# Value products of attention in two 64-query halves with the 64 columns of the own head, and input panels up to 512 columns wide

## What is computed

```python
# mixers of the first block (shortened)
p = rms_norm(x, mix_norm) @ w_in            # 512 x 2208
na:   softmax over a neighbourhood (mask and bias), q and k normed per head
mla:  latents -> w_uq, w_ukv -> heads of 96, rope on 32 of them
diff: w = softmax(q1 k1 + bias) - lam * softmax(q2 k2 + bias), per head
gqa:  4 query heads, 2 key/value heads, axial rope
out = einsum('bhqk,bkhd->bqhd', p, v)       # the value product of each head
```

## Time and profile before

| | |
|---|---|
| median of three runs | 2552.68 us (2552.34 to 2555.12) |
| profiled execution | 2552.25 us, its span 2550.5 us |
| PE, PEld, DVE, ACT busy | 97%, 80%, 51%, 36% of the span |
| projection, layers 0 and 1 | 376.03 to 503.53, 1449.67 to 1576.28 |
| attention, layers 0 and 1 | 503.53 to 672.97, 1576.28 to 1745.15 |

### The profile page before, as it was taken

How to read it: one execution, slowest core, us unless ns; L and a number is a source line. 1 busy time by engine, 2 the same in 40 slices (tenths; PEclk the granted TensorE clock), 3 DMA queues, 4 the chain that set the end, 5 groups by cost and what they waited for, 6 DMA issues and landing times.

```text
span 2550.5 us, 35687 instructions
## 1 busy us (share of the span) xinstructions
PE 2467.1 (97%) x14276; PEld 2041.9 (80%) x14276; DVE 1301.8 (51%) x2078; ACT 920.7 (36%) x1399; POOL 20.5 (1%) x14
## 2 busy tenths in 40 slices
PE   8999999999999999999999999999999999999898
PEld 7888889866778888888888898667788888778686
DVE  5434453468654344564344453785543446573464
ACT  4222233466432222332222335664321224343522
POOL 1000000000000000010000000000000000000000
PEclk9999999999999999999999999999999999999989
DMA  7333233100133333342332321002333324221001
GB/s 218 89 101 99 83 106 94 44 8 10 50 83 94 96 100 88 101 132 84 106 99 81 109 77 44 18 1 66 83 88 102 102 82 135 81 85 50 1 8 62
DMA packets 330945, 201.42 MB, mean 79 GB/s; under 512 B 9872, under 2 KB 328304, under 8 KB 330448
## 3 DMA queue, kind: packets, MB, share of 16 engines
q1 hardware_dynamic: 330288, 195.68, 26.6%
q0 software_dynamic: 544, 4.18, 0.5%
HBM read 197.74 MB, written 2.10 MB: 78 GB/s over the span
## 4 chain that ended last, share of the span: by engine, by line
PE 88%; DVE 5%; ACT 3%; DVEq 2%; issue 1%; DMA 0%; ACTq 0%; SPq 0%
PE bank L863 71%; PE bank L1056 3%; PE bank L1089 3%; PE bank L1029 2%; PE bank L1042 2%; PE bank L1337 1%; PE bank L980 1%; DVE w_lo L1995 1%; ACT w_hi L1486 0%; PE bank L992 0%; DVE top L2367 0%; DMA raw<-in_ffn_w_gate 0%; PE bank L1404 0%; DVEq L2389 0%; DVE bank L2373 0%
## 5 line engine op out<-in xcount | busy, mean ns | idle before, releaser
L863 PE MATMUL bank<-h_hi,w_hi 128*128 128x512 f32 x1640 | 642.9, 392 | 9.6 <-DVE h_lo L2006 5.9
L863 PE MATMUL bank<-h_hi,w_lo 128*128 128x512 f32 x1640 | 639.8, 390 | 0.0
L863 PE MATMUL bank<-h_lo,w_hi 128*128 128x512 f32 x1640 | 639.7, 390 | 0.0
L1995 DVE TENSOR_TENSOR w_lo<-raw,w_hi 128x2048 fp32r<-128x2048 f32 (+2 forms) x198 | 408.3, 2062 | 206.2 <-ACT w_hi L1486 204.1
L1486 ACT CAST w_hi<-raw 128x2048 fp32r<-128x2048 f32 (+2 forms) x198 | 340.2, 1718 | 383.4 <-PE bank L863 347.9
L863 PEld LDWEIGHTS bank<-h_hi,w_hi 128*128 128x128 f32 x1640 | 308.9, 188 | 82.6 <-issue 12.1
L863 PEld LDWEIGHTS bank<-h_hi,w_lo 128*128 128x128 f32 x1640 | 308.7, 188 | 64.7
L863 PEld LDWEIGHTS bank<-h_lo,w_hi 128*128 128x128 f32 x1640 | 308.9, 188 | 63.6 <-issue 0.2
L1527 ACT ACTIVATE probs<-probs 128x512 f32<-128x512 f32 x88 | 55.6, 632 | 680.7 <-DVE probs L2088 680.7
L863 PE MATMUL bank<-hid_hi,w_hi 128*128 128x512 f32 x704 | 273.9, 389 | 0.0
L863 PE MATMUL bank<-hid_lo,w_hi 128*128 128x512 f32 x704 | 273.9, 389 | 0.0
(11 more groups left out here) (413 smaller groups left out, 2701.4 us busy)
## 6 DMA issues: line engine op xcount, KB each, us to landing
raw<-in_ffn_w_gate SPq DMA_DIRECT2D x88, 512.0 KB, 4.0
raw<-in_ffn_w_up SPq DMA_DIRECT2D x88, 512.0 KB, 5.2
raw<-in_w_in SPq DMA_DIRECT2D x64, 512.0 KB, 4.6
raw<-in_ffn_w_down SPq DMA_DIRECT2D x64, 384.0 KB, 3.9
raw<-in_ffn_w_down SPq DMA_DIRECT2D x64, 320.0 KB, 3.3
raw<-in_w_out SPq DMA_DIRECT2D x24, 512.0 KB, 4.5
na_bias<-in_na_rel POOLq DMA_DIRECT2D x2, 1792.0 KB, 9.9
wide<-in_x SPq DMA_DIRECT2D x2, 1024.0 KB, 6.2
```

The source lines that it names most:

```text
L863: last = pe.matmul(to, left[a](k), right[b](k), start=(k == 0 and a + b == 0), stop=(k == n - 1 and a == 1))
L1995: dve.tensor_tensor(w_lo[:, at, 0:n], raw[:, at, 0:n], w_hi[:, at, 0:n].bitcast(F32), ALU.subtract)\
```

## The change

*Panels.* `IN_BLOCKS` has five blocks of up to 512 columns (four of 512, one of 416; the last joins `NA_V` and `DF_V`). Each is loaded and used as two panels of 4 row tiles (`KB`), still ten panels in all. PE adds both panels of a block in bank t, so that bank t is held over two panels, and ACT copies 512 (416) columns once per block. In ACT's order the copies of turns and the roots now stand ahead of the copies of the panel, and the split of panel n + 2 waits by itself until PE has done panel n. In DVE's order `seg_scale` stands ahead of the split. The products of the first panel need row tiles 0 to 3 alone.

*Value products.* `weigh` makes each product as two, with 64 queries stationary each, written to partitions 0 to 63 and 64 to 127 of the bank; only the 64 columns of the own head move. Results lie where they lay.

```diff
-IN_CHUNKS = [(NA_QK, PW), (NA_QK + PW, PW), (GQ_QK, PW), (GQ_QK + PW, PW), (C_Q, PW), (C_Q + PW, B_IN - PW),
-             (DF_QK, PW), (DF_QK + PW, PW), (NA_V, PW), (DF_V, PW)]
+IN_BLOCKS = [[(NA_QK, 2 * PW)], [(GQ_QK, 2 * PW)], [(C_Q, B_IN)], [(DF_QK, 2 * PW)], [(NA_V, PW), (DF_V, PW)]]
+N_IN = 2 * len(IN_BLOCKS)
+N_COPY = len(IN_BLOCKS) * T
+KB = KD // 2
...
@@ pe, project
+                        if part == 0 and block:
+                            pe.wait_ge(proj_copied, at_layer(l, N_COPY, (block - 1) * T + t + 1))
+                        product(bank[t][:, 0:w], h_parts(slice(t * P, (t + 1) * P), part * KB),
+                                w_parts(slot(l, i), KB, w, slice(None)), KB,
+                                operand(l, 1) + part * KB if block == 0 and t == 0 else None,
+                                begin=(part == 0), end=(part == 1)).then_inc(proj_done, 1)
-                        if m == 1:
+                        if m == 2:
                             sums_of_squares(norm_at(l, MIX_NORM))
...
+            def weigh(to, share, value, begin, end):
+
+                for half in range(2):
+                    last = pe.matmul(to[half * HD:(half + 1) * HD], share[:, half * HD:(half + 1) * HD], value, start=begin, stop=end)
+                return last
...
@@ pe, attention
-                                last = pe.matmul(bank[PAIR_MIXED][:, j * P:(j + 1) * P],
-                                                 pair_probsT(p)[:, j, t * P:(t + 1) * P],
-                                                 values(mixer, heads[j], t), start=(t == 0), stop=(t == T - 1))
+                                o = j * P + value_half(mixer, heads[j])
+                                last = weigh(bank[PAIR_MIXED][:, o:o + HD], pair_probsT(p)[:, j, t * P:(t + 1) * P],
+                                             values(mixer, heads[j], t), t == 0, t == T - 1)
...
@@ act, project: behind the turn copies and the roots
+                    for t in range(T) if part else ():
+                        act.wait_ge(proj_done, at_layer(l, N_PROJ, n * T + t + 1))
+                        o = 0
+                        for a, w in IN_BLOCKS[block]:
+                            last = act.activation(proj[:, t, a:a + w], bank[t][:, o:o + w], ACT.Copy, scale=rstd_tok[:, t:t + 1])
+                            o += w
+                        last.then_inc(proj_copied, 1)
+                    if n + 2 < N_IN:
+                        act.wait_ge(proj_done, at_layer(l, N_PROJ, (n + 1) * T))
+                        split(l, PAN_IN + n + 2, KB * IN_WIDTH[(n + 2) // 2])
...
```

More of the change, by code:

```diff
@@ L767, in _ @@
                 load_ffn(l, 1)
-                for n, piece in enumerate(IN_CHUNKS):
-                    load_columns(l, PAN_IN + n, A["w_in"], [piece])
+                for n in range(N_IN):
+                    load_columns(l, PAN_IN + n, A["w_in"], IN_BLOCKS[n // 2], n % 2 * KB, KB)
                 take(l, PAN_LAT)
@@ L852, in spread_roots, with product @@
                 last.then_inc(spread_done, 1)
-            def product(to, left, right, n, ready=None, hid=None):
+            def product(to, left, right, n, ready=None, hid=None, begin=True, end=True):
                 for k in range(n):
@@ L862, in product, with h_parts @@
                     for a, b in ((0, 0), (0, 1), (1, 0)):
-                        last = pe.matmul(to, left[a](k), right[b](k), start=(k == 0 and a + b == 0),
-                                         stop=(k == n - 1 and a == 1))
-                return last
-            def h_parts(cut=slice(None)):
-                return [lambda k, x=x: x[:, k, cut] for x in (h_hi, h_lo)]
+                        last = pe.matmul(to, left[a](k), right[b](k), start=(begin and k == 0 and a + b == 0),
+                                         stop=(end and k == n - 1 and a == 1))
+                return last
+            def h_parts(cut=slice(None), k0=0):
+                return [lambda k, x=x: x[:, k0 + k, cut] for x in (h_hi, h_lo)]
             def w_parts(at, k, n, cut, a=0):
@@ L932, in project @@
             def project(l):
-                for n, (a, w) in enumerate(IN_CHUNKS):
-                    i = PAN_IN + n
+                for n in range(N_IN):
+                    i, w, (block, part) = PAN_IN + n, IN_WIDTH[n // 2], divmod(n, 2)
                     for t in range(T):
@@ L1592, in project @@
                 act.drain()
[L1593 to L1600 removed]
+                for n in range(N_IN):
+                    block, part = divmod(n, 2)
                     for t in range(T):
@@ L2257, in project @@
             def project(l):
-                for n in range(len(IN_CHUNKS)):
-                    if n + 2 < len(IN_CHUNKS):
-                        split(l, PAN_IN + n + 2, KD * IN_CHUNKS[n + 2][1])
+                for n in range(N_IN):
                     for g in GROUPS:
```

42 lines of the change are left out of this document (16 added, 26 removed).

## The result

| | before | after |
|---|---|---|
| median of 4 runs, us | 2553.80 | 2508.95 |
| lowest to highest, us | 2552.34 to 2555.12 | 2506.54 to 2510.63 |
| profiled execution (span), us | 2552.25 (2550.5) | 2510.63 (2508.8) |
| projection, layer 0 / 1, us | 127.50 / 126.61 | 116.31 / 115.10 |
| attention, layer 0 / 1, us | 169.48 / 168.89 | 159.86 / 159.51 |

The ratio is 0.9824, with a 95% interval from 0.9807 to 0.9841: 1.8% faster, where 1.8% was forecast (2507). The kernel before has one more execution here (2554.91) than stood ahead of the prediction. Stage lengths are distances between first matmuls of stages. The stages in the table give back 43.4 us of the span; 2.2 us of that are lost in the first feed-forward, where this execution had 3.4 us of half clock from 28.4, ahead of all that the change touches.

What follows compares the result with a forecast made beforehand. TensorE (PE) was taken as the bound, with a matmul in flight for 97% of the span. Projection 22.7, attention 21.2 and L1244 1.5 sum to 45.4 us; 2552.25 less that gives 2506.9, forecast 2507, range 2498 to 2517 (0.60).

Steps and rivals of the forecast that it cites:

- Prices: Projection matmuls, start to start: 0.2266 us for 512 columns, 0.1866 for 416; wider panels save 9.5 us per layer.
- Projection, 11.4 and 11.3 us less: Input projection of layers 0 and 1: cheaper matmuls and fewer waits save 22.7 us together, bounds 18 to 28.7.
- The stall: Projection, ahead of panel 6: PE idles about 3.3 us until DVE's subtraction, which stands behind the gqa scaling.
- Pairs: Attention value products: a two-head pair saves 0.55 or 0.70 us, a `diff` pair 0.28 or 0.13, after drains.
- Attention, 10.6 us less: Attention, per layer: 12.6 us of halves' gain comes through, less two more clock falls of 1.0 each; 21.2 over both.
- Steps 17 to 25: Attention from 572 to 613, PE and DVE each waiting for the other: 1.2 of 3.6 us comes through.
- steps 26 to 38: Attention from 613 to 657, PE busy 43.8 of 44 us, DVE 33.9: 3.8 of 5.0 us comes through.
- L1244: Value products of one attention of the second block: 1.5 us saved, bounds -1 and 2.
- Swallowed: Rival, attention: DVE swallows PE's gain, leaving 22.7 and at most 8 us; 2522 to 2530 us, chance 0.17.
- All of it: Rival, whole change: no projection stall or fall (28.7), PE's full 35.8 in attention, 2.0 more; 2486 us, chance 0.11.
- Halves in turn: Rival, value products: halves follow one another, 0.43 us per product instead of 0.2233; 2642 us, chance 0.05.
- The clock: Rival, attention: clock stays at half rate, some 80 us a layer for half of attention; 2590 us, chance 0.03.

Runs made afterwards that it cites:

- e6: Changed kernel with each 512 (416) column projection product issued as two matmuls of 256 and 256 (256 and 160) columns: 2515.87 us, ratio 0.9856.
- e3: Changed kernel with DVE's subtraction for panel 6 made after the first of four gqa token tiles instead of after all four: 2499.34 us, ratio 0.9789.
- e11: Changed kernel with both edits, each wide product as two matmuls and panel 6's subtraction after the first gqa token tile: 2515.39 us, ratio 0.9848.
- e5: Changed kernel, but attention issues all key tiles of the first 64 queries, then all of the other 64: 2524.13 us, ratio 0.9884.
- e1: Changed kernel with value products of full width as before; panels and new ACT and DVE orders stay: 2529.52 us, ratio 0.9905.
- e2: Kernel before with value products in halves alone, panels untouched: 2531.08 us, ratio 0.9916.
- e8: Changed kernel, value products in halves, with the gain product and rotation of mla's q and k left out on DVE: 2486.09 us, ratio 0.9742.
- e7: Changed kernel with full-width value products as in e1 and the gain product and rotation of mla's q and k left out: 2514.14 us, ratio 0.9845.
- e4: Changed kernel, each value product as one with 128 queries stationary and only the own head's 64 columns moving: 2537.74 us, ratio 0.9929.

## Why the prediction was right, point by point

- **Prices.** 512 columns 0.2267 (0.2266 said), 416 columns 0.1889 (0.1866 said, on a straight line between rows). Right, and e6 shows that the price is a matter of matmuls' number: two for one costs 114.3 - 105.2 = 9.1 us a layer by these steps, 8.8 us as measured.
- **Projection, 11.4 and 11.3 us less.** 11.2 and 11.5. The stall was 3.3 by hand and 2.87 idle in the trace, with the releaser that was named; the half clock was 444.8 to 451.6, as long as before. Layer 1 had half of it, 3.4 us at 1499.5, as it had before. That the clock fell at all, and for as long, was the dearest case in layer 0: behind the same stall it cost nothing, 1.5 or 2.8 us in other traces (see the order on DVE), so hitting 116.3 there is in part luck. e3 took both away and left 5.1 us beside the matmuls' 105.2; the working had 11.2 - 3.3 - 3.0 = 4.9. So the terms are shown, not only the total. What the working did not say is that the stall hangs on the width: without the width there is no stall either (e6, e11), so of the 9.5 us of cheaper matmuls the changed kernel keeps 2.9 and 4.1.
- **Pairs.** 1.15 for 32 matmuls was said and found; a two-head step is 0.56 shorter, 0.55 was said, and the 0.25 allowed for two drains is borne out twice, by 4.20 - 0.80 + 0.25 = 3.65 (3.64 measured) and by e5's step, 4.20 - 0.41 + 0.25 = 4.04 (503.00 to 507.04 in its timeline). `diff` steps save 0.15 (3.42 to 3.27), 0.13 was said.
- **Attention, 10.6 us less.** It was 9.6 and 9.4; this is the term that was mis-sized. In layer 0, steps 3 to 9 gave 3.7 (3.9 said), 10 to 16 gave 2.4 (2.0), the rest behind step 39 gave 1.4 (1.2). Steps 17 to 25 gave -0.5; 1.2 had been said there, less 2.0 for two more clock falls of 3.4 us. That makes -0.8, and the nearness is luck, for neither part holds. The falls came (6.8 + 3.4 us at 0.50 for 3.4 before), but not from the halves: e1, with full width, had the same 6.8 + 3.4 us there, and e2, with halves, had 3.4. Nor did they lengthen these steps once the products were halves: they took 41.17 at 0.96 (e2) and at 0.88 (the changed kernel) alike, with DVE setting most of the pace; with full width the same 10.2 us of half clock went with 1.0 us more (e1). And the 1.2 us of halves did not come there: at 3.4 us of half clock these steps took 40.64 before and 41.17 in e2. With a light DVE the nine steps gave 0.9 and all of attention 0.4 to 1.6 us more, although e8 had 3.4 us of half clock there (559.5) and e7 none. Why the steps got half a microsecond longer no run shows. Two more steps of the working failed. The half microsecond at the start, from copies that ACT no longer makes, didn't come: 8.31 in both. And steps 26 to 38 gave 2.7, not 3.8. Windows of that stretch, before and, behind it, after:

```profile
612.88:637.65 24.77, 24.77 (x158) 17.93 (x156) 18.31 (x51) 16.73 (x40) 0.00 (x0) 1.00 0.00 1
637.65:657.24 19.59, 19.40 (x121) 13.79 (x121) 15.75 (x40) 13.28 (x31) 0.00 (x0) 1.00 0.01 1
```

```profile
598.32:620.95 22.63, 22.48 (x241) 14.22 (x237) 17.64 (x49) 16.59 (x40) 0.00 (x0) 1.00 0.01 2
620.95:640.01 19.06, 17.84 (x189) 10.69 (x185) 16.47 (x42) 13.29 (x31) 0.00 (x0) 1.00 0.01 2
```

  PE's busy time fell by 3.85 us (44.17 to 40.32), which is what was said. The time fell by 2.7, for PE now idles 1.37 us in it instead of 0.19. Nearly all of that is one wait, ahead of the transposes of one pair, for DVE's scaled probabilities; the view of waits for this stretch of the changed kernel has one line (before, the same wait was 0.2):

```profile
PE bank L1052 <- DVE spare_hi L2374: 1.1, 1, 1.1
```

  I had taken a DVE share of 33.9 in 44 as room enough. It is an average, and the step in which DVE was late stood inside it.
- **L1244.** 1.5 us was said with 2 as the bound. From the first to the last of its products it took 22.1 us before (2352.7 to 2374.8) and 19.7 us after (2313.6 to 2333.3): 2.4, just outside. The stretch from the end of layer 1's attention to the last matmul, in which they lie, became only 1.7 us shorter. Which of its deductions was too large no run tells.
- **Rivals.** Swallowed: no, 9.5 of 10.6 came. All of it: no. That rival put 28.7 us on projections without stall or fall, but 28.7 leaves the stall in (22.7 and two times 3.0 for the clock); by the working's own terms it is 35.3, and e3, without either, gave 33.4. Halves in turn: the trace of e5 refutes the rival's price more than its mechanism. It took 0.107 for each matmul of a half, from a product with 128 stationary columns; within one column group they stand 0.058 apart, so even wholly in turn the four would take 0.23 for a product of 0.223: with the drains, a total near that of the kernel before (an estimate from these rows) and not 2642. e5, which takes a part of the overlap away, was still faster than e1. The nearest row was the wrong one: e4 shows that it is the stationary side that costs. The rule of the Trainium skill ("TensorE: Matmul & The Clock Gate", Part 3, The mechanism), by which a load overlaps only where row groups differ, doesn't hold for what is measured here: all rows in both groups, different columns, and two series of loads and matmuls at once. Before the change, too, loads of full width were under way for 23.27 of 32.00 us in which PE was never idle. Another place of that page (Part 1, Architectural detail) has matmuls of one sub-array run while another still loads its weights; this case's rows fit that one.
- **The clock.** Attention's granted clock is 0.97, where it was 0.99: 6.8 us more of half clock in layer 0 (two falls of 3.4, as allowed), not the long one of the rival, and most of it in steps where it cost little. e4's 23.9 us of half clock show that the rival was no idle one.

## What to carry to other kernels

Price an edit on the busiest engine together with the engine that will be late next: here three lines of order on DVE were worth 9.6 us by the medians, but only once the products were fast, and the same order was worth nothing with slow ones. When only half of the moving columns is used, cutting them alone gained nothing (e4); what gained was to split the stationary side as well and put the two halves beside each other. After making PE faster, look for its idle times: here one of 2.9 us cost 3.1, and half clock behind it up to 2.8 more. Where another engine sets the pace, half clock on PE cost little or nothing, so price a clock fall by the slack that PE has there.

## What the runs showed of the hardware

- Matmuls of 64 stationary and 64 moving columns, all 128 rows, start 0.058 us apart in one column group, and the two groups run together: 32 of them in 1.15 us, 0.0300 a pass (1.15 less 0.22, over 31), against 0.112 for a pass with 128 stationary and 128 moving columns. With eight of one group ahead of eight of the other the second series started 0.29 us behind the first, and 32 took 1.54 us.
- With 128 stationary columns, 64 moving columns save next to nothing (1.90 for 1.95 us in 16 matmuls).
- 256 and 160 columns back to back take 0.230, with 0.154 from the wide start to the narrow one and 0.075 from the narrow to the next wide; 416 in one matmul take 0.189.
- Going from full width to 64-column tiling and back cost 0.24 us in a two-head step: the products became 0.80 us shorter, the step 0.56.
- In the changed kernel the clock fell to 0.50 at 444.8, within PE's idle time of 2.87 us, and at 564.3, between idle times of 2.36 and 0.88 us, each time for 6.8 us; in e4 it stayed there for 13.7 us in which PE was busy throughout.
- Behind 14 idle times of 2.83 to 2.88 us at the same place of the program the clock was at 0.50 for 6.8 us three times, for 3.4 us eight times, and not at all three times.
